# A convolution's taps and a pair of sines in the order of a mixer's work on Trainium2

## The reference

```
p = h @ w_in                                   # 1024 -> 8192 columns
q = _rope(heads(rq, RET_HEADS), positions)     # needs sin and cos of the positions
k = _rope(heads(rk, RET_HEADS), positions) * (RET_HEAD_DIM ** -0.5)
o = _retention(q, k, heads(rv, RET_HEADS))     # 4 heads, then normed and gated
o = _hgrn2(silu(gq), logf, -expm1(logf), gi)   # 4 heads, then normed and gated
u = _causal_dwconv(ca * sigmoid(cb), conv_w, conv_b)   # 512 channels, 31 taps
u_c = silu(layer_norm(u))
y = sum over the three branches of sigmoid(gate) * (u_branch @ w_branch)
return y @ w_out
```

## Time and profile before

| | us |
|---|---|
| median of 3 runs (lowest, highest) | 3453.51 (3451.85, 3455.03) |
| the profiled execution's own time | 3449.65 |
| its span, first to last instruction | 3447.8 |
| PE busy | 3301.4 (96%) |
| DVE busy | 2119.4 (61%) |
| ACT busy | 1323.5 (38%) |
| POOL busy | 620.4 (18%) |

### The profile page before, as it was taken

The page is one execution under the profiler, slowest core; times in us unless marked ns, Lnnn a source line. Parts: engine busy times, 40 slices in busy tenths (PEclk is TensorE's granted clock), DMA queues, the critical chain, the costliest instruction groups (busy, mean ns, idle before and its releaser), DMA issues. The chain is left out here.

```text
span 3447.8 us, 38741 instructions
## 1 busy us (share of the span) xinstructions
PE 3301.4 (96%) x15264; PEld 2645.9 (77%) x15264; DVE 2119.4 (61%) x2693; ACT 1323.5 (38%) x1716; POOL 620.4 (18%) x496
## 2 busy tenths in 40 slices
PE   8899999999999999998999998999899999989997
PEld 6577788886677788876788776888677887768886
DVE  8854566448753666457766646554677666465545
ACT  4664322234663322234332334332443332343323
POOL 2212222121212213111000232010210002320002
PEclk9999999999999999999999999999999999999999
DMA  3122455322123545231111222222222112322221
GB/s 131 42 68 79 174 196 195 122 98 67 47 71 102 195 192 191 94 115 67 68 68 68 92 93 91 94 97 97 81 79 74 61 62 92 104 74 98 98 94 65
DMA packets 72180, 344.43 MB, mean 100 GB/s; under 512 B 25152, under 2 KB 26048, under 8 KB 35648
## 3 DMA queue, kind: packets, MB, share of 16 engines
q1 hardware_dynamic: 70416, 339.12, 28.2%
q0 software_dynamic: 576, 2.33, 0.2%
q10 hardware_dynamic: 1008, 0.51, 0.1%
HBM read 340.51 MB, written 2.10 MB: 99 GB/s over the span
## 5 line engine op out<-in xcount | busy, mean ns | idle before, releaser
L897 PE MATMUL bank<-Hhi_b,whi_b 128*128 128x512 f32 x2976 | 1206.3, 405 | 68.7 <-ACT Hhi_b L2053 22.1
L898 PE MATMUL bank<-Hhi_b,wlo_b 128*128 128x512 f32 x2976 | 1165.0, 391 | 0.0
L904 PE MATMUL bank<-Hlo_b,whi_b 128*128 128x512 f32 x2976 | 1155.4, 392 | 0.9 <-DVE Hlo_b L2325 0.8
L875 DVE TENSOR_TENSOR wlo_b<-raw_b,whi_b 128x2048 fp32r<-128x2048 f32 (+2 forms) x290 | 622.5, 2147 | 480.2 <-ACT whi_b L869 479.9
L897 PEld LDWEIGHTS bank<-Hhi_b,whi_b 128*128 128x128 f32 x2976 | 562.5, 189 | 214.3 <-issue 41.6
L904 PEld LDWEIGHTS bank<-Hlo_b,whi_b 128*128 128x128 f32 x2976 | 560.2, 189 | 123.9 <-DVE Hlo_b L2325 4.9
L898 PEld LDWEIGHTS bank<-Hhi_b,wlo_b 128*128 128x128 f32 x2976 | 562.7, 189 | 119.7 <-issue 9.1
L869 ACT ACTIVATE whi_b<-raw_b 128x2048 fp32r<-128x2048 f32 (+2 forms) x290 | 511.8, 1765 | 364.8 <-PE bank L904 361.4
L897 PE MATMUL bank<-Uhi_b,whi_b 128*128 128x512 f32 x1024 | 405.6, 396 | 4.3 <-POOL Ulo_b L986 4.3
L898 PE MATMUL bank<-Uhi_b,wlo_b 128*128 128x512 f32 x1024 | 399.8, 390 | 0.0
L904 PE MATMUL bank<-Ulo_b,whi_b 128*128 128x512 f32 x1024 | 386.4, 391 | 0.0
(11 more groups left out here) (255 smaller groups left out, 3422.0 us busy)
## 6 DMA issues: line engine op xcount, KB each, us to landing
raw_b<-in_w SPq DMA_DIRECT2D x234, 1024.0 KB, 4.9
ada_b<-in_wada SPq DMA_DIRECT2D x48, 1024.0 KB, 6.9
raw_b<-in_w SPq DMA_DIRECT2D x40, 512.0 KB, 3.6
raw_b<-in_w SPq DMA_DIRECT2D x16, 768.0 KB, 4.2
rel_b<-in_rel SPq DMA_DIRECT2D x128, 24.0 KB, 2.4
X_keep<-in_x SPq DMA_DIRECT2D x4, 512.0 KB, 9.2
decay_b<-in_decay POOLq DMA_DIRECT2D x2, 1024.0 KB, 6.6
out<-X_keep SPq DMA_DIRECT2D x8, 256.0 KB, 2.0
```

What stands on the lines that cost most here:

```text
L875: self.nc.vector.tensor_tensor(self.wlo[n % RAW_SLOTS][:, 0:words], self.raw[n % RAW_SLOTS][:, 0:words], self.whi[n % HI_SLOTS][:, 0:words ...
L897: self.nc.tensor.matmul(out, whi[:, k, cols], xhi, start=(k == 0), stop=False)
L898: self.nc.tensor.matmul(out, wlo[:, k, cols], xhi, start=False, stop=False)
L904: mm = self.nc.tensor.matmul(out, whi[:, k, cols], xlo, start=False, stop=(k == nk - 1))
```

## The change

Three edits to the list's order; the instructions themselves stay, all of them.

1. `TAPS_FIRST`: in layer one, the panels with the indices 1 and 2 have no free taps beside them. (Index 0 is worked in one go and never had any.)
2. The item `sines` moves from in front of panel 2 to behind its first piece, which is behind `round` and `rest` of panel 3.
3. `taps_beside` allows none where a group holds an `orec` behind something else, and allows one beside even levels instead of odd ones. Level 0 shares its group with the transposed values and has none, so a head has 3 taps beside its levels where it had 4.

```
@@ taps_beside @@
     if kinds[0] in ("cross", "hpv"):
         return 1
+    if "orec" in kinds:
+        return 0
     if kinds[0] == "level":
-        return group[0][4] % 2
+        return 1 - group[0][4] % 2
     return 1 if group[0][2] == "r" else 0
 
 
 MIX_FROM = (0, 4, 8)
+TAPS_FIRST = (0, 0, 0)
@@ schedule_two @@
-            if l == 0 and i == 2:
-                s.add("sines")
...
                     if l == 0 and i == 1 and j == 0:
                         s.add("setup")
+                    if l == 0 and i == 2 and j == 0:
+                        s.add("sines")
                     if i <= len(heads + gates):
-                        gap(3 if kind == "z" else 2)
+                        gap(TAPS_FIRST[i] if l == 0 and i < len(TAPS_FIRST) else 3 if kind == "z" else 2)
```

## The result

| | before | after |
|---|---|---|
| median (lowest, highest), us | 3453.00 (3451.85, 3455.03), 4 runs | 3434.04 (3433.20, 3435.53), 4 runs |
| the profiled execution's own time | 3449.65 | 3435.53 |
| its span | 3447.8 | 3433.7 |

The ratio is 0.9945, with a 95% interval of 0.9928 to 0.9962: 19 us less, where 12.4 were forecast. In all that follows, lines of the changed kernel have numbers 3 above those of before; in the other kernels the offset differs by a line or more.

What follows compares the result with a forecast made beforehand. TensorE, busy 3301.4 of 3447.8 us, was taken as the bound, so only what starts or delays its matmuls counts. Terms -9.8 - 3.4 + 0.8 = -12.4 us gave 3441.1 us from the median 3453.51; range 3436.5 to 3446.5.

Steps and rivals of the forecast that it cites:

- The start: Fourth panel of layer one's mixer: wait 1.3 instead of 9.30 us and 1.80 of low clock saved, -9.8 us.
- so their waits do too: Attention values: the order of the work that makes them stays, so TensorE's waits there stay; no gain counted.
- The levels' waits: Level 2's multiplied keys, HGRN heads 1 to 3 of each layer: six waits each shrink by 0.57, -3.4 us.
- The rival in which the taps land on the levels' path: Taps behind levels 2, 4 and 6 delay DVE's multiplications: 18.0 us lost, sum +9.0, 3462.5 us; chance 0.02.
- The displaced taps: Three taps in front of HGRN head 0's gating product in layer one take 3.4 us: 0.8 us lost.
- the clock's: Low clock at the fourth panel: twelve matmuls take 2.73 instead of 4.53 us, 1.80 counted as saved.
- half of it comes back: Behind 1556 us, later waits or four low-clock pieces of 1.8 us return 7.2: -5.2, 3448.3 us; chance 0.06.
- the same chance in the other direction: Luckier clock behind 1556 us, with less low clock at later waits: 3437.5 us; chance 0.06.
- The rope: Rope becomes the wait: fourth panel at 1558.0, 2.1 us wait, low clock again; sum -9.8, 3443.7 us; chance 0.17.
- Level taps give nothing: Level keys wait for the reciprocal or new tap, so the 3.4 is lost: -9.0, 3444.5 us; chance 0.12.
- slower: 24 taps behind levels 2, 4 and 6 delay TensorE's level products: +9.0, 3462.5 us; chance 0.02.
- The sines come later: Table switch holds ScalarE 1.4 us longer, moving the fourth panel's wlo: sum -11.0, 3442.5 us; chance 0.04.

Runs made afterwards that it cites:

- the further edits: Changed kernel with score product before keys' rotation, head 0's rotations behind the fourth panel's low half, three taps later, two late panels with more taps: 3424.92, again 3424.21 us.

## Why the prediction was wrong, step by step

**The start: right in size, wrong in cause.** Forecast -9.8, with a wait of 1.3 us; measured 1.35, and -9.6 in the first row of the table. The -9.6 has parts that the sum did not have so: -8.2 for the wait, -1.1 of low clock where 1.8 was forecast, and -0.4 at the value product at the end of that stretch (2.14 and 2.15 us before, 1.77 after), less 0.1 of other waits. The forecast had ruled that last one out ("so their waits do too"). In before's profile the keys' sine product starts 0.28 us behind GpSimd's cosine product and takes 1.78 us; in the changed kernel's it starts 0.08 us ahead of it and takes 0.69. All profiles with the first three panels free of taps have the shorter wait. The forecast also said of the taps' removal that "this alone wouldn't do, because ScalarE's order still puts the sines before whi". It does: 3441.58 and 3441.44 us with the taps alone, 3442.01 with both. I had worked out a path through ScalarE for the new order and not for the old one with the taps gone. In the old order `whi` ends at 1554.27 in that trace, and VectorE gets to `wlo` only at 1555.31, so it was covered. The forecast times hold to 0.2 us once they are moved by 3.1: 2.1 that program one took longer in this execution and 1.0 of longer low clock in the first panels. `wlo` was put at 1554.8 and started at 1557.96, the panel at 1557.2 and 1560.35.

**The levels' waits: right.** Forecast -3.4 for six waits, measured -3.8. The rival in which the taps land on the levels' path fell: no wait at levels 4, 6 or the cross products.

**The displaced taps: right.** Forecast +0.8 at HGRN head 0 of layer one, measured +0.67 at the wait. Some of it comes back: the levels' row of layer one is 0.3 us shorter in the three profiles with the start's edit and odd levels (148.8) than without it (149.1).

**The step that failed is the clock's.** The forecast charged low clock in one place, behind the wait of 9.30 us, and took it as fixed everywhere else. The waits' terms give -9.6 - 3.8 + 0.4 = -13.0 us; the three profiles of the changed kernel against the two of before give -17.5. The missing 4.5 us are -0.8, -0.9, -1.7 and -1.1 in the second, fifth, sixth and last row of the table (the fifth less 0.1 of other differences). In three of them, 3.6 us, it is low clock that before paid and the changed kernel mostly did not, and all but the second stand behind waits that no edit changed; the fifth is the mixed one. Over the five profiles, TensorE's idle time in program two falls by 12.7 us and the busy time of the same matmuls by 4.9, where the sum had 10.6 and 1.8. The forecast had this as the rival "half of it comes back", with "the same chance in the other direction", at 0.06 and 3437.5 us, two such pieces. It was the side that came, with between two and three; the medians, 17.8 to 19.0 us apart in the groups, have up to one more. The range could not have held it by its own working either: the forecast less the spread of 1.6 is 3439.5, and none of the cases that it names for the range leads down to 3436.5.

What the 20 profiles show of it. Behind the waits of 1.93 to 1.95 us at level 3, low clock followed in 4 of 18; behind the 22 that the even levels have there, 1.29 to 1.32 us, in none. Behind layer one's value product the wait of 2.12 to 2.15 us was followed by it in 3 of 5, and that of 1.77 to 1.81 in none of 9. These counts suggest a direct effect, fewer drops behind shorter waits, but of the 4.5 us only the second row's 0.8 can be that. And length alone is not the measure: behind the layer norms' waits of 1.58 to 1.60 us, which have a pause of 0.26 to 0.28 us shortly before and most often one behind, low clock followed in 34 of 40 cases, in layer two in all but four profiles, two of them of the changed kernel (that is the last row of the table). Behind layer two's value product, with 2.12 to 2.16 us in all 14 profiles that have the wait, it followed in 6, five of which have odd levels in layer one and four the long first wait; all three of the changed kernel are without it. There the wait is the same and the outcome isn't. Whether an earlier shift of the program decides that was tried with the two kernels that have the levels' edit in one layer, and neither had it. Why it goes one way or the other stays open.

**The other rivals.** The rope did become the last piece in front of the fourth panel, with 1.35 us and not 2.1, and without low clock. "Level taps give nothing" and "slower" had no sign in the traces. "The sines come later" had a drain behind the table load as its cause. The Trainium skill (ScalarE: Activation LUTs, "What ACT_TABLE_LOAD costs") states one of about 1.38 us. Here the load takes 1.28 us and the cosine starts 1.29 us after the load's start (1551.10 and 1552.39 in the rows above); the trace doesn't agree.

## What to carry to other kernels

Price a wait of TensorE at its length, and let the range hold low clock on either side of that, also behind waits that the change doesn't touch: here 12.7 us less of waiting came with 17.5 us, and 8.6 us less, in the further edits, with 8.6. Before a gain is put down to two edits, follow each engine's list with only one of them made. Filler work that is moved has to be followed to its end: three taps left without a place cost 2.1 us of wait and 1.6 us of clock at the far end of the layer, and at most 0.4 us a few panels earlier.

## What the runs showed of the hardware

- Two waits of the same length at the same place, 2.12 and 2.13 us, were followed by low clock in some executions and kernels and not in others; each time it cost 1.6 to 1.8 us. A wait of 1.58 to 1.60 us with a short pause before it was followed by it in 34 of 40 cases, one of 1.77 to 1.81 without it in none of 9. Executions of one kernel differ by several such pieces.
- A rope or table operation on VectorE costs two to three times as much or a little more beside GpSimd's products: 1.40 instead of 0.43 us for a table operation, 1.37 and 1.78 instead of 0.69 for a product. Moving the sines only changed which of them paid.
